# Norm squares summed by VectorE, an earlier memory load, and dt computed by feature in a three-layer float32 kernel

## The chip, the cores and the metric

The kernel runs on one core of one Trainium2 chip. The metric is the device time of one execution in microseconds (us); lower is better. TensorE multiplies, VectorE, ScalarE and GpSimd do the elementwise work, and SyncE issues the transfers. The profile calls them PE (with PEld for its weight loads), DVE, ACT, POOL and SP.

## The reference

The input is x, 512 tokens of 1024 features, and two memories of 256 tokens. A first block adds three branches to the residual stream h, each after an RMS norm: a mixer (a projection, a causal convolution of width 4, a chunked state space scan with 16 heads, and a multi-scale pooling), a cross attention on the memory, and a SwiGLU feed-forward. Two more layers (a convolution layer and a sparse attention layer) follow a final norm. All is float32.

```python
def rmsnorm(x, g):
    xf = x.astype(jnp.float32)
    y = xf * lax.rsqrt(jnp.mean(xf * xf, axis=-1, keepdims=True) + EPS)
    return (y * g.astype(jnp.float32)).astype(x.dtype)
...
    proj = u @ w_in
    z, xbc, dt_raw, v = jnp.split(
        proj, [SSD_INNER, SSD_INNER + CONV_DIM, SSD_INNER + CONV_DIM + SSD_HEADS], axis=-1)
...
    dt = jax.nn.softplus(dt_raw.astype(jnp.float32) + dt_bias.astype(jnp.float32))
...
    for l in range(DEPTH):
        h = h + hybrid_mixer(rmsnorm(h, mix_norm[l]), w_in[l], conv_w[l], conv_b[l], dt_bias[l],
                             a_log[l], d_skip[l], ssd_norm[l], pool_w[l], pool_scale[l], w_out_mix[l])
        h = h + memory_cross_attention(rmsnorm(h, xattn_norm[l]), rmsnorm(mem, mem_norm[l]),
                                       w_q[l], w_kv[l], w_o[l])
        h = h + swiglu(rmsnorm(h, ffn_norm[l]), w_gate_up[l], w_down[l])
    return rmsnorm(h, final_norm)
```

## The kernel before

The stream h is kept transposed in hT: features on the 128 partitions, 8 tiles of 512 tokens. Every large product is done in split precision. A weight tile of 1024 rows and 256 columns (1 MB) is loaded into w_raw in two halves, GpSimd splits it into w_hi (one instruction, L613) and w_lo (four, L628), and TensorE multiplies w_hi by the high part of the input, w_hi by its low part and w_lo by its high part. Such a tile with its products is a job. Jobs are numbered in one list, JOBS, and run strictly in that order: kv1_k (4), kv1_v (4), xbc (6), dt (1), v (4), z (4), pool (1), wo_pool (4), wo_ssd (4), q1 (4) and so on.

There are two slots for weights. SyncE loads tile j once tile j-2 is split (slot_free), GpSimd splits tile j once job j-2 has been used up (w_used), and TensorE starts job j once tile j is split (w_split) and the output bank of job j-2 has been emptied (g_free). A job with 512 tokens has 48 matmuls of 512 columns, one on the memory 48 of 256 columns. products_as_ready (L711) is the form that takes its input tile by tile as the low part appears; products_T (L698) and products_nat (L720, output by token) take it whole. The other results of TensorE go through four banks of t_bank in the order of the list TASKS.

The opening: SyncE issues 21 small parameter transfers into p_rows, then mem (1 MB), then x (2 MB), then three broadcasts, then the weight tiles of kv1_k. ScalarE waits for mem and all parameters, squares mem for its norm (L1185), VectorE scales mem (L1794), TensorE transposes it, ScalarE writes m_hi and VectorE m_lo (L1802), which counts m1_lo. TensorE then transposes x (L796), sums the squares of x (statistic, L752), and only then runs the kv1_k jobs.

The norm of h needs the sum over all 1024 features, that is over partitions as well. ScalarE squares each of the 8 tiles into a ring of two buffers (nring), and TensorE multiplies a matrix of ones by each square, accumulating: 8 tiles, each of which the trace shows as two float32 matmuls. For the first norm that is L752, for the other three (stat2, stat3, stat4) squares_sum (L766), two tiles after each output job and the last two after the first job of the next stage. ScalarE takes the root, VectorE the reciprocal and applies it.

The dt job is a product by token with only 16 columns: x is the stationary operand, in 96 matmuls of 16 columns. VectorE turns its output into dt and adt, and then runs the four pooling windows (window, L1853 to L1869), for which the v jobs deliver the input.

Of the kernel before, what the change touches and what calls it, by code (L numbers as in the profile page):

```python
# [20 lines left out]
ALU = mybir.AluOpType  # L21
ACT = mybir.ActivationFunctionType
# [4 lines left out]
P = 128  # L27
D = 1024
DT = D // P
T = 512  # L30
# [89 lines left out]
def slot_tasks(s):  # L120
# [7 lines left out]
    [("params", 2), ("mem1", 4), ("x", DT), ("stat1", 1), ("xbcT", XS + GROUPS), ("acs", 1), ("cb", 2), ("abc0", 4)]  # L128
# [62 lines left out]
def program(nc, A, out):  # L191
    with ExitStack() as ctx:
        def sem(name):
            return ctx.enter_context(nc.semaphore(name))
# [48 lines left out]
        mean = at("mean", [P, T], rN + 2 * KB)  # L243
        nring = at("nring", [P, 2, T], rN + 4 * KB)
# [28 lines left out]
        dt_, adt, acs, eacs, dtd, cdec = sm  # L273
        t1, t2, t3 = [at(n, [P, CHUNKS, HEADS], rM + 8 * KB + 256 * i) for i, n in enumerate(("t1", "t2", "t3"))]
# [116 lines left out]
        xs_ready = sem("xs_ready")  # L391
        dtx, sp_e, sp_l, adt_ready = sem("dtx"), sem("sp_e"), sem("sp_l"), sem("adt_ready")
# [43 lines left out]
        def _(sp):  # L436
# [26 lines left out]
            for s, rows in enumerate(PARAM_SETS):  # L463
                r = 0
                for name, arr, n in rows:
                    if len(A[arr].shape) == 1:
                        v = A[arr].rearrange("(r c) -> r c", c=P)
                    elif len(A[arr].shape) == 2:
                        v = A[arr].rearrange("a (r c) -> (a r) c", c=P)
                    else:  # L470
                        v = A[arr].rearrange("a t (r c) -> (a t r) c", c=P)
                    if s >= 2:
                        v = v[(s - 2) * n:(s - 1) * n, :]
                    sp.dma_start(p_rows[r:r + n, s, :], v).then_inc(in_small, 16)
                    r += n
# [4 lines left out]
            stream(JOBS["kv1_k"], 4, w_cols("w_kv", 0))  # L480
# [203 lines left out]
        def _(pe):  # L684
# [72 lines left out]
            def sq(k):  # L757
                return nring[:, k % 2, :]

            def squares_sum(i, nth, k0, k1):  # L760

                if k0 == 0:
                    bank(i)
                for k in range(k0, k1):
                    pe.wait_ge(sq_ready, nth * DT + k + 1)
                    last = nc.tensor.matmul(t_bank[:, BANK[i], :], ones[:], sq(k), start=(k == 0), stop=(k == DT - 1))  # L766
                    if k < DT - 1:
                        last.then_inc(sq_used, 1)
                    else:
                        last.then_inc(t_ready, 1)  # L770
# [21 lines left out]
            pe.wait_ge(in_x, 16)  # L792
            for k in range(DT):
                b = bank(TASKS["x"] + k)
                for m in range(TT):
                    last = nc.tensor.transpose(b[:, m * P:(m + 1) * P], x_nat[:, m, k * P:(k + 1) * P], ident[:])  # L796
                last.then_inc(t_ready, 1)
            statistic(TASKS["stat1"], DT, sq, (sq_ready, 0), sq_used)
# [112 lines left out]
            for i in range(1, 4):  # L911
                jobs(JOBS["wo_ssd"] + i, 1, lambda par: products_T(par, x_hi, x_lo))
                squares_sum(TASKS["stat2"], 1, 2 * i - 2, 2 * i)
            products_as_ready(JOBS["q1"], y_hi, y_lo, lambda k: pe.wait_ge(nlo_ready, DT + k + 1))
            squares_sum(TASKS["stat2"], 1, 6, 8)
# [40 lines left out]
            for i in range(1, 4):  # L956
                jobs(JOBS["wo1"] + i, 1, lambda par: products_T(par, y_hi, y_lo))
                squares_sum(TASKS["stat3"], 2, 2 * i - 2, 2 * i)

            products_as_ready(JOBS["gu0"], x_hi, x_lo, lambda k: pe.wait_ge(nlo_ready, 2 * DT + k + 1))  # L960
            squares_sum(TASKS["stat3"], 2, 6, 8)
            f0 = 0
            for c, n in enumerate(FF_CHUNKS):
                first = 1 if c == 0 else 0
                jobs(JOBS[f"gu{c}"] + first, n - first, lambda par: products_T(par, x_hi, x_lo))
                products_as_ready(JOBS[f"down{c}"], y_hi, y_lo, lambda k: pe.wait_ge(ff_lo, f0 + k + 1), kt=n)
                if c < 2:
                    jobs(JOBS[f"down{c}"] + 1, 3, lambda par: products_T(par, y_hi, y_lo, kt=n))
                else:
                    for i in range(1, 4):  # L970
                        jobs(JOBS[f"down{c}"] + i, 1, lambda par: products_T(par, y_hi, y_lo, kt=n))
                        squares_sum(TASKS["stat4"], 3, 2 * i - 2, 2 * i)
                f0 += n
            jobs(JOBS["kvb_k"], 1, lambda par: products_T(par, m_hi, m_lo, n=MEM))
            squares_sum(TASKS["stat4"], 3, 6, 8)
# [168 lines left out]
        def _(act):  # L1144
# [17 lines left out]
            def squares(n, used0, ready_wait):  # L1162
                for k in range(n):
                    ready_wait(k)
                    if k >= 2:
                        act.wait_ge(sq_used, used0 + k - 1)
                    nc.scalar.activation(nring[:, k % 2, :], hT[:, k, :], ACT.Square).then_inc(sq_ready, 1)

# [11 lines left out]

            act.wait_ge(in_mem1, 16)
# [23 lines left out]
            for k in range(DT):  # L1205
                i = TASKS["x"] + k
                b = ready(i)
                copy(hT[:, k, :], b).then_inc(h_tile, 1)
                act.wait_ge(h_tile, k + 1)
                act.nop().then_inc(t_free[BANK[i]], 1)  # L1210
            squares(DT, 0, lambda k: None)
            root(TASKS["stat1"])

# [3 lines left out]

            for i in range(4):
                norm_hi(0, 2 * i)
                norm_hi(0, 2 * i + 1)  # L1220
                j = JOBS["kv1_k"] + i
                act.wait_ge(w_used, j + 1)
                copy(k1[:, 2 * i:2 * i + 2, :], g_bank[:, 2 * (j % 2):2 * (j % 2) + 2, 0:MEM]).then_inc(g_free[j % 2], 1)
            for i in range(4):
# [61 lines left out]

            act.wait_ge(dtx, 1)
# [3 lines left out]
            raw_pair(0, JOBS["v"])  # L1291
# [65 lines left out]
            def square(nth, k):  # L1357
                if k >= 2:
                    act.wait_ge(sq_used, nth * (DT - 1) + k - 1)
                nc.scalar.activation(nring[:, k % 2, :], hT[:, k, :], ACT.Square).then_inc(sq_ready, 1)  # L1360
# [363 lines left out]
        def _(dve):  # L1724
# [35 lines left out]
            def add_to_residual(base, n=4):  # L1760

                for i in range(n):
                    j = base + i
                    dve.wait_ge(w_used, j + 1)
                    for f in range(2):
                        k = 2 * i + f
                        ins = v.tensor_tensor(hT[:, k, :], hT[:, k, :], g_bank[:, 2 * (j % 2) + f, :], ALU.add)  # L1767
                        if f == 0:
                            ins.then_inc(h_done, 1)
                        else:  # L1770
                            done(ins, h_done, g_free[j % 2])

# [33 lines left out]
            dve.wait_ge(t_ready, TASKS["x"] + DT)  # L1806
# [3 lines left out]
            dve.wait_ge(h_tile, DT)  # L1810
# [17 lines left out]
            j = JOBS["dt"]  # L1828
            dve.wait_ge(w_used, j + 1)
            g = g_bank[:, 2 * (j % 2):2 * (j % 2) + 2, :].rearrange("p b (m c) -> p (b m) c", c=WC)[:, :, 0:HEADS]  # L1830
            done(v.tensor_tensor(t3[:], g, bc[:, 0:1, :].to_broadcast([P, CHUNKS, HEADS]), ALU.add), g_free[j % 2])
# [192 lines left out]

            def residual_and_lo(base, nth, gain, hi, lo):

                for i in range(4):
# [9 lines left out]
                    for k in (2 * i, 2 * i + 1):  # L2037
                        dve.wait_ge(nhi_ready, nth * DT + k + 1)
                        v.scalar_tensor_tensor(lo[:, k, :], hT[:, k, :], gain(k), hi[:, k, :].bitcast(F32),
                                               ALU.mult, ALU.subtract).then_inc(nlo_ready, 1)  # L2040

# [44 lines left out]
            for c, n in enumerate(FF_CHUNKS):  # L2086
# [13 lines left out]
                add_to_residual(JOBS[f"down{c}"])  # L2100
# [300 lines left out]
```

## Time and profile before

| | |
|---|---|
| median of 3 runs | 1885.59 us (1884.83 to 1888.43) |
| profiled execution | 1885.64 us, its span 1883.6 us |
| mean granted TensorE clock | 0.972 of full speed |
| busy: PE, DVE, ACT, POOL | 94%, 50%, 27%, 57% |

The span is the time between the first and the last instruction that the profiler saw, and 2.0 us lie around it. Times in rows are counted from the span's start.

### The profile page before, as it was taken

The numbers are of one execution on the slowest core, as the hardware profiler recorded it, in microseconds if no ns is written. First come the engines' busy times: TensorE is split into PE (matmuls) and PEld (weight loads), VectorE is DVE, ScalarE is ACT, GpSimd is POOL, SyncE is SP. The second block draws the span as 40 slices with busy tenths as digits, with TensorE's granted clock in tenths as the row PEclk, the third lists the DMA queues.
The fourth block names the chain that finished last, engine by engine and source line by source line (L and its number), as shares of the span: only waits on it lengthen the run. The fifth ranks groups of instructions, "written<-read, shape, count | busy, mean of one in ns | idle before, by whom it ended". The sixth has DMA issues, their size and how long they took to land.

```text
span 1883.6 us, 23072 instructions
## 1 busy us (share of the span) xinstructions
PE 1769.3 (94%) x8317; PEld 1433.4 (76%) x8317; DVE 937.1 (50%) x1455; ACT 514.2 (27%) x876; POOL 1077.5 (57%) x781
## 2 busy tenths in 40 slices
PE   4899999899999999999999999998898989999995
PEld 3778897687787788888878877875676768777783
DVE  2547674665232331221219998997314676452313
ACT  4122223232031210110112435645102234554103
POOL 3976664236554666666777787672762544334550
PEclk9998999899999999999999999999898999999998
DMA  4332222112232233333234332221231222121211
GB/s 163 112 112 69 68 90 67 45 68 67 92 130 57 80 111 90 89 112 90 78 102 128 95 89 90 68 89 46 67 82 43 90 68 68 45 68 45 90 45 45
DMA packets 188503, 153.14 MB, mean 81 GB/s; under 512 B 9412, under 2 KB 186112, under 8 KB 188416
## 3 DMA queue, kind: packets, MB, share of 16 engines
q1 hardware_dynamic: 188416, 151.95, 26.0%
q8 instruction: 58, 0.95, 0.2%
q14 instruction: 29, 0.24, 0.0%
HBM read 148.79 MB, written 2.10 MB: 80 GB/s over the span
## 4 chain that ended last, share of the span: by engine, by line
PE 77%; DVE 12%; issue 5%; ACT 3%; POOL 2%; DMA 1%; DVEq 1%; SPq 0%; ACTq 0%; POOLq 0%
PE g_bank L698 49%; PE g_bank L711 7%; PE g_bank L720 6%; DVE t_bank L2145 4%; PE t_bank L752 2%; PE t_bank L1102 1%; PE t_bank L1092 1%; PE t_bank L888 1%; POOL w_lo L628 1%; PE t_bank L766 1%; PE g_bank L1046 1%; PE t_bank L838 1%; POOL w_hi L613 1%; DVE isc L2285 1%; PE t_bank L934 1%
## 5 line engine op out<-in xcount | busy, mean ns | idle before, releaser
L628 POOL TENSOR_TENSOR w_lo<-w_raw,w_hi 128x512 fp32r<-128x512 f32 x480 | 653.9, 1393 | 10.0
L613 POOL TENSOR_SCALAR w_hi<-w_raw 128x2048 fp32r<-128x2048 f32 x120 | 244.5, 2038 | 668.5 <-issue 292.7
L698 PE MATMUL g_bank<-x_hi,w_hi 128*128 128x512 f32 x1248 | 494.3, 396 | 3.0 <-DVEq L1738 3.0
L698 PE MATMUL g_bank<-x_hi,w_lo 128*128 128x512 f32 x1248 | 487.1, 390 | 0.0
L698 PE MATMUL g_bank<-x_lo,w_hi 128*128 128x512 f32 x1248 | 487.1, 390 | 0.0
L698 PEld LDWEIGHTS g_bank<-x_hi,w_hi 128*128 128x128 f32 x1248 | 235.1, 188 | 55.2 <-issue 7.4
L698 PEld LDWEIGHTS g_bank<-x_lo,w_hi 128*128 128x128 f32 x1248 | 235.1, 188 | 49.7 <-issue 1.7
L698 PEld LDWEIGHTS g_bank<-x_hi,w_lo 128*128 128x128 f32 x1248 | 234.9, 188 | 49.3
L2145 DVE SCALAR_TENSOR_TENSOR t_bank<-hc,cols,t_bank 128x512 f32<-128x512 f32 x280 | 186.2, 747 | 2.4 <-DVE hc L2123 2.4
L646 POOL TENSOR_TENSOR w_lo<-w_raw,w_hi 128x512 fp32r<-128x512 f32 x80 | 100.9, 1294 | 63.9 <-ACT w_hi L1457 63.9
L698 PE MATMUL g_bank<-y_hi,w_hi 128*128 128x512 f32 x332 | 132.1, 398 | 1.4 <-ACTq L1326 1.4
L698 PE MATMUL g_bank<-y_hi,w_lo 128*128 128x512 f32 x332 | 129.4, 390 | 0.0
L698 PE MATMUL g_bank<-y_lo,w_hi 128*128 128x512 f32 x332 | 129.3, 390 | 0.0
L2235 DVE SCALAR_TENSOR_TENSOR hT<-hT,g_bank 128x512 f32<-128x512 f32 x32 | 20.5, 683 | 131.7 <-PE g_bank L698 111.9
L2092 DVE TENSOR_TENSOR gs<-g_bank,rstd 128x512 f32<-128x512 f32 x22 | 15.2, 691 | 140.2 <-PE g_bank L698 140.0
L1435 ACT ACTIVATE sg<-gs 128x512 f32<-128x512 f32 x22 | 13.9, 632 | 253.7 <-DVE gs L2092 253.7
L698 PEld LDWEIGHTS g_bank<-y_hi,w_hi 128*128 128x128 f32 x332 | 62.4, 188 | 15.9 <-issue 2.8
L698 PEld LDWEIGHTS g_bank<-y_lo,w_hi 128*128 128x128 f32 x332 | 62.4, 188 | 13.8 <-issue 1.2
L698 PEld LDWEIGHTS g_bank<-y_hi,w_lo 128*128 128x128 f32 x332 | 62.3, 188 | 13.1
L662 POOL TENSOR_TENSOR pacc<-pacc,prod 128x512 f32<-128x512 f32 x54 | 68.2, 1296 | 5.9 <-ACT prod L1146 5.9
L1767 DVE TENSOR_TENSOR hT<-hT,g_bank 128x512 f32<-128x512 f32 x24 | 15.4, 684 | 99.0 <-PE g_bank L698 82.0
L2311 DVE CUSTOM_DVE_ANT_0 pB<-t_bank,mask 128x128 f32<-128x128 f32 (+3 forms) x48 | 23.6, 491 | 76.4 <-PE t_bank L1092 69.0
(357 smaller groups left out, 2948.5 us busy)
## 6 DMA issues: line engine op xcount, KB each, us to landing
w_raw<-w_gate_up SPq DMA_DIRECT2D x44, 512.0 KB, 4.6
w_raw<-a_w_in SPq DMA_DIRECT2D x44, 512.0 KB, 4.4
w_raw<-b_w_in SPq DMA_DIRECT2D x38, 512.0 KB, 4.4
w_raw<-w_in SPq DMA_DIRECT2D x28, 512.0 KB, 4.3
w_raw<-w_kv SPq DMA_DIRECT2D x16, 512.0 KB, 4.3
w_raw<-w_out_mix SPq DMA_DIRECT2D x16, 512.0 KB, 4.4
w_raw<-w_down SPq DMA_DIRECT2D x16, 512.0 KB, 4.4
w_raw<-a_w_out SPq DMA_DIRECT2D x16, 512.0 KB, 4.1
```

Of the source, the lines that this page charges most:

```text
L613: nc.gpsimd.tensor_scalar(w_hi[:, par], w_raw[:, par], 1.0, 0.0, ALU.mult, ALU.add).then_inc(pool_chain, 1)
L628: last = nc.gpsimd.tensor_tensor(w_lo[:, par, s], w_raw[:, par, s], w_hi[:, par, s].bitcast(F32), ALU.subtract)
L646: last = nc.gpsimd.tensor_tensor(w_lo[:, par, s], w_raw[:, par, s], w_hi[:, par, s].bitcast(F32), ALU.subtract)
L662: nc.gpsimd.tensor_tensor(acc_k[:], acc_k[:], p[:], ALU.add).then_inc(tap_chain, 1)
L698: last = nc.tensor.matmul(g_bank[:, 2 * pair + f, 0:n], ww[:, par, k0 + k, ws], xk, start=(k == 0 and q == 0), stop=(k == kt - 1 and q == 2))
L711: last = nc.tensor.matmul(g_bank[:, 2 * par + f, :], ww[:, par, k, ws], xx[:, k0 + k, :], start=(k == 0 and q == 0), stop=(k == kt - 1 and ...
L720: last = nc.tensor.matmul(g_bank[:, 2 * par + m // 2, m % 2 * WC:m % 2 * WC + n], xx[:, k, m * P:(m + 1) * P], ww[:, par, k, 0:n], start=( ...
L752: last = nc.tensor.matmul(b, ones[:], src(k), start=(k == 0), stop=(k == n - 1))
L766: last = nc.tensor.matmul(t_bank[:, BANK[i], :], ones[:], sq(k), start=(k == 0), stop=(k == DT - 1))
L2145: ins = v.scalar_tensor_tensor(tail if k == TAPS - 1 else a(k), h(k), wk, a(k), ALU.mult, ALU.add)
L2235: ins = v.scalar_tensor_tensor(hT[:, k, :], hT[:, k, :], 1.0 if half else ALPHA, g_bank[:, 2 * (j % 2) + f, :], ALU.mult, ALU.add)
L2311: ins = v.tensor_tensor_reduce(p_unit(u, i), b[:, i % per * W_OF[1]:i % per * W_OF[1] + w], mask[:, M_AT[qb]:M_AT[qb] + w], SLOPES[4 * hg ...
```

## The change

1. The memory is transferred first, then the weight tiles of kv1_k jobs 0 and 1, then x and the broadcasts; SyncE issues these. The 21 parameter transfers are issued by ScalarE's queue.
2. TensorE's order is kv1_k 0 and 1, the transposes of x tiles 0 to 3, kv1_k 2, x tiles 4 to 7, kv1_k 3, and the first norm's sum.
3. For all four norms ScalarE writes the first square to sq_sum and the others to the ring; VectorE adds the seven others to sq_sum, and TensorE does one product of ones with sq_sum. For stat2, stat3 and stat4 it stands where the last two tiles' products stood.
4. dt is computed by feature: w (16 columns) is the stationary operand and x moves, in 24 matmuls of 512 columns; ScalarE copies the 16 rows to dtT, and behind the first v job TensorE transposes them back (four transposes, task dtT). ScalarE's evacuation of the first v job stands ahead of its two dt activations.

```diff
-    [("params", 2), ("mem1", 4), ("x", DT), ("stat1", 1), ("xbcT", XS + GROUPS), ("acs", 1), ("cb", 2), ("abc0", 4)]
+    [("params", 2), ("mem1", 4), ("x", DT), ("stat1", 1), ("xbcT", XS + GROUPS), ("dtT", 1), ("acs", 1), ("cb", 2), ("abc0", 4)]
...
             sp.dma_start(mem1[:], A["mem"][0].rearrange("(m p) d -> p m d", p=P)).then_inc(in_mem1, 16)
+            k_cols = w_cols("w_kv", 0)
+            for i in range(2):
+                load(i, i, k_cols(i * WC))
             sp.dma_start(x_nat[:], A["x"][0].rearrange("(m p) d -> p m d", p=P)).then_inc(in_x, 16)
...
+            def squares_sum(i, nth):
+
+                b = bank(i)
+                pe.wait_ge(sq_used, (nth + 1) * (DT - 1))
+                nc.tensor.matmul(b, ones[:], sq_sum[:], start=True, stop=True).then_inc(t_ready, 1)
...
             pe.wait_ge(m1_lo, DT)
-            jobs(JOBS["kv1_k"], 4, lambda par: products_T(par, m_hi, m_lo, n=MEM))
+            kv1_k(0)
+            kv1_k(1)
+            x_T(0, 4)
+            kv1_k(2)
+            x_T(4, 8)
+            kv1_k(3)
+            b = bank(TASKS["stat1"])
+            pe.wait_ge(sq_used, DT - 1)
+            nc.tensor.matmul(b, ones[:], sq_sum[:], start=True, stop=True).then_inc(t_ready, 1)
...
-            jobs(JOBS["dt"], 1, lambda par: products_nat(par, x_hi, x_lo, TT, n=HEADS))
+            j = JOBS["dt"]
+            slot(j, j % 2, j // 2)
+            for k in range(KT):
+                for q, (ww, xx) in enumerate(((w_hi, x_hi), (w_hi, x_lo), (w_lo, x_hi))):
+                    last = nc.tensor.matmul(g_bank[0:HEADS, 2 * (j % 2), :], ww[:, j % 2, k, 0:HEADS], xx[:, k, :],
+                                            start=(k == 0 and q == 0), stop=(k == KT - 1 and q == 2))
+            last.then_inc(w_used, 1)
...
-            jobs(with_v, 2, lambda par: products_T(par, x_hi, x_lo))
+            jobs(with_v, 1, lambda par: products_T(par, x_hi, x_lo))
+            pe.wait_ge(dt_moved, 1)
+            b = bank(TASKS["dtT"])
+            for c in range(CHUNKS):
+                last = nc.tensor.transpose(b[:, c * HEADS:(c + 1) * HEADS], dtT[0:HEADS, c * P:(c + 1) * P], ident[0:HEADS, 0:HEADS])
+            last.then_inc(t_ready, 1)
+            jobs(with_v + 1, 1, lambda par: products_T(par, x_hi, x_lo))
...
+            for k in range(1, DT):
+                dve.wait_ge(sq_ready, k + 1)
+                v.tensor_tensor(sq_sum[:], sq_sum[:], nring[:, k % 2, :], ALU.add).then_inc(sq_used, 1)
+                dve.wait_ge(sq_used, k)
...
+            def add_squares(nth, i):
+
+                for k in (2 * i, 2 * i + 1):
+                    dve.wait_ge(sq_ready, nth * DT + k + 1)
+                    if k:
+                        v.tensor_tensor(sq_sum[:], sq_sum[:], nring[:, k % 2, :], ALU.add).then_inc(sq_used, 1)
+                        dve.wait_ge(sq_used, nth * (DT - 1) + k)
```

## Rows read from the trace of the kernel before

**Rows 1.** The page's head and its first part (busy us, share, instructions).

```profile
span 1883.6 us, 23072 instructions
PE 1769.3 (94%) x8317; PEld 1433.4 (76%) x8317; DVE 937.1 (50%) x1455; ACT 514.2 (27%) x876; POOL 1077.5 (57%) x781
```

**Rows 2.** The chain that ended last, opening (start us, us, what).

```profile
32.69 9.06 PE t_bank L752 x16
41.75 9.96 PE g_bank L698 x84
...
103.26 11.23 PE g_bank L711 x48
```

**Rows 3.** Timeline of POOL, opening: tiles 1, 3 and 9.

```profile
26.05 1.90 POOL L613 TENSOR_SCALAR w_hi<-w_raw 128x2048 fp32r<-128x2048 f32 x1 [21.91 <-DMA w_raw<-w_kv]
...
47.70 2.31 POOL L613 TENSOR_SCALAR w_hi<-w_raw 128x2048 fp32r<-128x2048 f32 x1 [7.82 <-PE g_bank L698]
...
98.19 5.02 POOL L628 TENSOR_TENSOR w_lo<-w_raw,w_hi 128x512 fp32r<-128x512 f32 x4
```

**Rows 4.** Timeline of the opening on SP, PE, ACT and DVE.

```profile
8.44 0.41 SPq L476 DMA_DIRECT2D mem<-mem  x1
11.91 0.98 PE L778 MATMUL t_bank<-ident,p_rows 116*128 116x116 f32 x4 [11.91 <-DMA p_rows<-a_conv_w]
14.24 1.06 ACT L1185 ACTIVATE x_hi<-mem 128x1024 fp32r<-128x1024 f32 x1 [1.11 <-DMA mem<-mem]
18.41 1.42 DVE L1794 TENSOR_SCALAR mem<-mem,mstat 128x1024 f32<-128x1024 f32 x2
26.33 1.11 DVE L1802 SCALAR_TENSOR_TENSOR m_lo<-t_bank,cols,m_hi 128x256 fp32r<-128x256 f32 x2 [0.32 <-DVE m_lo L1802]
68.60 3.47 DVE L1788 TENSOR_TENSOR x_lo<-nring,x_hi 128x512 fp32r<-128x512 f32 x2
```

**Rows 5.** DMA issues (issues, KB each, median us to landing).

```profile
w_raw<-w_kv SPq DMA_DIRECT2D x16, 512.0 KB, 4.3
mem<-mem SPq DMA_DIRECT2D x2, 1024.0 KB, 5.4
```

**Rows 6.** Timeline of DVE: one instruction with POOL splitting, and without.

```profile
115.21 1.67 DVE L1823 TENSOR_SCALAR acc<-raw,cols 128x512 f32<-128x512 f32 x1 [43.14 <-ACT raw L1146]
...
170.39 0.53 DVE L1823 TENSOR_SCALAR acc<-raw,cols 128x512 f32<-128x512 f32 x1
```

**Rows 7.** The chain, dt job, v jobs 0 and 1, v jobs 2 and 3.

```profile
174.68 17.97 PE g_bank L720 x96
192.65 24.23 PE g_bank L698 x96
...
217.28 21.86 PE g_bank L698 x96
```

**Rows 8.** Windows, dt job (busy us of PE, PEld, DVE, ACT, POOL; PEclk; DMA share; GB/s).

```profile
178.00:182.00 4.00, 4.00 (x20) 4.00 (x21) 3.93 (x3) 0.00 (x0) 4.00 (x3) 0.50 0.00 0
```

**Rows 9.** Timeline of DVE: end of adt, first and last row of the four windows.

```profile
200.22 0.23 DVE L1842 SCALAR_TENSOR_TENSOR adt<-dt__95,bc 128x64 f32<-128x64 f32 x1
206.71 0.08 DVE L1853 MEMSET wbuf<- 128x30 f32 x1 [6.27 <-ACT raw L1146]
...
261.56 1.48 DVE L1869 TENSOR_TENSOR y_lo<-acc,y_hi 128x512 fp32r<-128x512 f32 x2
```

**Rows 10.** The chain, stat2: two pairs of tiles and a 512-token job.

```profile
436.77 1.96 PE t_bank L766 x4
438.73 10.91 PE g_bank L698 x48
449.63 1.72 PE t_bank L766 x4
```

**Rows 11.** Timeline of POOL, second kvb_k tile, and the chain, first a_glu job.

```profile
980.27 1.90 POOL L613 TENSOR_SCALAR w_hi<-w_raw 128x2048 fp32r<-128x2048 f32 x1 [2.90 <-issue]
1012.95 11.34 PE g_bank L711 x48
```

More of the change, by code:

```diff
@@ L479, in _ @@
                 sp.dma_start(bc[:, i, :], A[n][0].partition_broadcast(P)).then_inc(in_bc, 16)
-            stream(JOBS["kv1_k"], 4, w_cols("w_kv", 0))
+            for i in range(2, 4):
+                slot_free(i)
+                load(i, i % 2, k_cols(i * WC))
             stream(JOBS["kv1_v"], 4, w_cols("w_kv", D))
@@ L791, in _, with x_T, kv1_k @@
                 last.then_inc(t_ready, 1)
[L792 to L798, printed above, removed]
-            pe.wait_ge(m1_lo, DT)
-            jobs(JOBS["kv1_k"], 4, lambda par: products_T(par, m_hi, m_lo, n=MEM))
+            def x_T(k0, k1):
+                pe.wait_ge(in_x, 16)
+                for k in range(k0, k1):
+                    b = bank(TASKS["x"] + k)
+                    for m in range(TT):
+                        last = nc.tensor.transpose(b[:, m * P:(m + 1) * P], x_nat[:, m, k * P:(k + 1) * P], ident[:])
+                    last.then_inc(t_ready, 1)
+            def kv1_k(i):
+                j = JOBS["kv1_k"] + i
+                slot(j, j % 2, j // 2 if j >= 2 else None)
+                products_T(j % 2, m_hi, m_lo, n=MEM).then_inc(w_used, 1)
+            pe.wait_ge(m1_lo, DT)
+            kv1_k(0)
[7 more added lines that the diff above has]
+            nc.tensor.matmul(b, ones[:], sq_sum[:], start=True, stop=True).then_inc(t_ready, 1)
             jobs(JOBS["kv1_v"], 4, lambda par: products_nat(par, m_hi, m_lo, MT))
@@ L910, in _ @@
                 last.then_inc(t_ready, 1)
-            for i in range(1, 4):
-                jobs(JOBS["wo_ssd"] + i, 1, lambda par: products_T(par, x_hi, x_lo))
-                squares_sum(TASKS["stat2"], 1, 2 * i - 2, 2 * i)
+            jobs(JOBS["wo_ssd"] + 1, 4 - 1, lambda par: products_T(par, x_hi, x_lo))
             products_as_ready(JOBS["q1"], y_hi, y_lo, lambda k: pe.wait_ge(nlo_ready, DT + k + 1))
-            squares_sum(TASKS["stat2"], 1, 6, 8)
+            squares_sum(TASKS["stat2"], 1)
             jobs(JOBS["q1"] + 1, 4 - 1, lambda par: products_T(par, y_hi, y_lo))
@@ L966, in _ @@
                 products_as_ready(JOBS[f"down{c}"], y_hi, y_lo, lambda k: pe.wait_ge(ff_lo, f0 + k + 1), kt=n)
[L967 to L972, printed above, removed]
+                jobs(JOBS[f"down{c}"] + 1, 3, lambda par: products_T(par, y_hi, y_lo, kt=n))
                 f0 += n
             jobs(JOBS["kvb_k"], 1, lambda par: products_T(par, m_hi, m_lo, n=MEM))
-            squares_sum(TASKS["stat4"], 3, 6, 8)
+            squares_sum(TASKS["stat4"], 3)
             jobs(JOBS["kvb_k"] + 1, 1, lambda par: products_T(par, m_hi, m_lo, n=MEM))
@@ L1204, in _, with k1_evac, x_and_squares @@
                     copy(m_hi[:, k, :], b[:, kk * MEM:(kk + 1) * MEM], col["mem_norm"](k)).then_inc(m1_hi, 1)
[L1205 to L1212, printed above, removed]
+            def k1_evac(i):
+                j = JOBS["kv1_k"] + i
+                act.wait_ge(w_used, j + 1)
+                copy(k1[:, 2 * i:2 * i + 2, :], g_bank[:, 2 * (j % 2):2 * (j % 2) + 2, 0:MEM]).then_inc(g_free[j % 2], 1)
+            def x_and_squares(k0, k1):
+                for k in range(k0, k1):
+                    i = TASKS["x"] + k
+                    b = ready(i)
+                    copy(hT[:, k, :], b).then_inc(h_tile, 1)
+                    act.wait_ge(h_tile, k + 1)
+                    act.nop().then_inc(t_free[BANK[i]], 1)
+                    if k >= 3:
+                        act.wait_ge(sq_used, k - 2)
+                    dst = nring[:, k % 2, :] if k else sq_sum[:]
+                    nc.scalar.activation(dst, hT[:, k, :], ACT.Square).then_inc(sq_ready, 1)
             def norm_hi(base, k):
@@ L1771, in add_to_residual @@
                             done(ins, h_done, g_free[j % 2])
+                    if nth is not None:
+                        add_squares(nth, i)
             def rms_apply(nth, gain):
```

91 lines of the change are left out of this document (42 added, 49 removed).

## The prediction

> **What bounds the kernel now.** I read the page's head first: PE is busy for 94% of the span, POOL for 57%, DVE for 50% [rows 1]. So work taken off TensorE counts where TensorE is the last to finish, and I went to the chain of waits to find where it isn't. In the opening the chain runs over the sum of squares, then kv1_k jobs 0 and 1, and it reaches the first xbc job at 103.26 [rows 2]. Between these TensorE needs only 6 us for a memory job, but POOL needs 7 us for a tile, and up to 9 where DVE works beside it. POOL's timeline shows that it started its third tile at 47.70, when kv1_k 0 had been used up, and ended the ninth, that of xbc 0, at 103.2: seven tiles in 55.5 us with one gap under 1 us [rows 3]. The opening is bound by POOL, and its clock starts with the first kv1_k job. From 103 us to the end of the feed-forward TensorE sets the pace in most places: a 512-token job takes 10.9 us [rows 10], a tile's split 7 to 8.5.
>
> **The opening (about 13 us less).** TensorE could not start kv1_k 0 before 41.75 - 0.6, because the transposes and squares of x stood ahead of it. Its own inputs were there earlier: m_lo was done at 27.4 [rows 4], and tile 0 was split only at 33 (26.05 and the 7 us of a split) because its weights stood behind mem, x and the broadcasts in SP's queue (POOL waited until 26.05) [rows 3].
> Afterwards mem is issued at about 0.8 in place of 8.44 [rows 4] and lands at 0.8 + 5.4 = 6.2 [rows 5]; tiles 0 and 1 follow it at some 4.3 us each [rows 5], so at about 11 and 15. Their splits take 7 us each: 11 to 18, 18 to 25.
> The parameters: SP issued 21 of them in 7.6 us, and the last landed at 11.9 [rows 4]. ScalarE's queue issuing such transfers is not in this trace; I take SP's price for it, so ScalarE can square mem at 12.0 in place of 14.24, 2.2 us earlier. From below the price is nothing; from above it is 0.6 us an issue (twice SP's), and then the parameters land at 16 and ScalarE starts 2 us later than before. Other transfers now run beside them, which pulls towards late.
> Against that, POOL now splits while DVE scales mem. DVE's one-input instruction took 1.67 us with POOL at work and 0.53 without [rows 6], 1.1 more; the two at L1794 [rows 4] and a small reciprocal then cost some 2.9 us in all. The m_lo instructions read a PSUM bank and one SBUF tensor, and the two at 26.33 took no longer with POOL splitting from 26.05 on [rows 3, 4]. So m_lo is done at 27.4 - 2.2 + 2.9 = 28.1, and TensorE starts there.
> The Trainium skill (SBUF - State Buffer, section "SBUF: two separate sides") says that the port pair of DVE and GpSimd is locked for a whole instruction by whichever comes first. The trace agrees, as the 1.67 against 0.53 us shows; without this rule the start would be 25.2 and the gain 3 us more.
> kv1_k 0 ends at 34.1, and POOL begins the third tile at 34.3, 13.4 us earlier than 47.70. Then seven tiles follow. As before, three of them run beside DVE's norm; the seven additions of squares touch two more, for which I add 0.5. So xbc 0 starts at 90, 13 us earlier. Is x ready? Tile transposes go between the kv1_k jobs. With splits at 41.3 and 49, kv1_k 3 ends near 56, the sum takes 0.9, and from the end of the sum to the last x_lo the kernel before took 72.1 - 41.75 = 30.3 us [rows 2, 4], so 87. That is 3 us of margin to 90, and products_as_ready gives 8 more. The weights of kv1_k 2 stand behind x and should land near 27, needed at 34.3. The removed part, seven of eight sums, lies off POOL's path and counts nothing here by itself. Bounds: 9 us (parameters late by 4) to 16.5 (no lock).
>
> **dt by feature (about 8 us less).** The job took 17.97 us [rows 7], at half clock (1.2 GHz) from 178 on [rows 8], with 16-column matmuls and PEld busy throughout. 24 matmuls of 512 columns cost 24/48 x 10.9 = 5.5 us [rows 10]. TensorE would reach v 0 at 180.1, but POOL has that tile split only at 182.0: it can start when xbc 5 has been used, at 173.8, ahead of the transposes before 174.68, and a split beside DVE takes some 8 us. So 10.6 us are left. v 0 and 1 took 24.23 where v 2 and 3 took 21.86 [rows 7]: the slow clock ran into them, and 2.4 us more come back. Transposes cost 0.3. That makes 12.7 us on TensorE.
> What is late next is DVE. Before, dt's small instructions were over at 200.4, and the windows waited for v 0 until 206.7 [rows 9]. Now v 0 is ready at 193.0, but dt's eight instructions come only behind the transposes and take the same 7.8 us, so the windows start at 201.5: 5.2 us earlier. They run 56.3 us nearly without a gap (206.7 to 263.0) [rows 9]; two gaps of 1.9 us in all, for which TensorE was late, close. ScalarE's copies of v wait for free ring buffers, and the z jobs wait for these copies, so the end of the windows sets z 2. I get 7 to 8.5 and take 8. Bounds: 4 (more lock time) and 12.7.
>
> **stat2, stat3, stat4 (7.4 + 6.0 + 3.7 us less).** Two tiles cost 1.72 us on TensorE, and there are 12 such pairs; the first one took 1.96, behind 1.1 of waiting for the square (the job ahead of it ended at 435.6) [rows 10]. One tile stays, 0.86 us. For stat2 that is 1.1 + 1.96 + 3 x 1.72 - 0.86 = 7.4, for stat3 4 x 1.72 - 0.86 = 6.0. DVE gets seven additions each. None of these stands in the trace; the nearest is a two-input instruction at 0.69 alone and up to 1.8 beside POOL. They stand behind the low parts that TensorE waits for. The last pair is done some 8 us after the last output job, and TensorE wants it after 10.9, so the cover is q1 0, gu0 0 or kvb_k 0. Without it the two last additions would cost 3.5 us each time. I take 0.
> For stat4 the cover matters: behind it come four memory tiles and POOL is last again, from 980.27 to a_glu 0 at 1012.95 [rows 11]. The first three pairs, 5.2 us, stand ahead of that run and let it start 3.5 us earlier (the tile before it, 7 us, is then the limit); the fourth is hidden. With the norm's apply a little more beside POOL I take 3.7. Bounds for all three: 11 to 18.5.
>
> **Sum.** 13 + 8 + 7.4 + 6.0 + 3.7 = 38.1. The profiled execution took 1885.64 us with a span of 1883.6, 0.05 over the median, so 1885.6 - 38.1 = 1847.5 us.
>
> **Rivals.** (a) Parameters late. The small transfers on ScalarE's queue share the engines with 3 MB of weights and mem and land at 16 or later; the opening gives 5 to 9, the total 30 to 34: 1851 to 1856. For it: this trace has no transfer that ScalarE issues. Against it: they are small.
> The Trainium skill (DMA: Bandwidth & Descriptors, "Issuing engines are not separate DMA queues") says that transfers from all issuers run on the same 16 engines and interleave, and that a second issuer saves only issue time. No run here shows it yet; by it alone the opening's gain would come from the order, and case (a) gets its chance.
> (b) dt gives TensorE's full 12.7 and the lock costs nothing: 38.1 + 4.7 + 3 = 46, 1840. For it: POOL splits fewer tiles at the places where DVE is late. Against it: rows 9.
> (c) The additions are exposed. DVE's sums come later than the cover, TensorE waits about 3.5 us in each of three norms and the first norm reaches xbc 0 late by 3: 14 less gain, 1861. Against it: 3 us of margin computed.
> (d) Slower than before. It has one mechanism: the squares of mem wait for parameters that land behind x. Everything in the opening moves with that landing. TensorE's start is 16 us behind it, so a landing at 25 us gives the opening's gain back, and slower than before needs one past 50. Before, mem, x and tile 0, 4 MB in all, were in at 26 us [rows 3].
>
> **How the numbers follow.** Main case 0.5, (a) 0.2, (b) 0.15, (c) 0.12, (d) and the like 0.03. The range 1837 to 1859 takes in (a) and (b) and the nearer half of (c), and leaves out 2 in 10. About 0.2% (3.8 us) is what a measurement of this kernel can tell from no change; faster by more has 0.96, within it 0.01, slower 0.03.
>
> **What would show it.** TensorE's first kv1_k matmul at 28 (25 if no lock, over 31 for case a); POOL's third tile at 34; xbc 0 at 90; x_lo done before that; the dt job 5.5 us at full clock with a short wait for POOL behind it; the windows starting 5 us earlier relative to the dt job; one pair of matmuls for each norm, with no wait ahead of it; a_glu 0 still behind POOL. The prediction is wrong if TensorE waits for x_lo at xbc 0, if the 16-column product lowers the clock as the old one did, or if ScalarE's issues take over 0.6 us each.

## The result and the profile after

The changed kernel takes 1858.68 us (median of 4 runs, 1857.81 to 1861.51) against 1886.61 us for the kernel before on the same chip (4 runs, 1884.83 to 1888.43): a ratio of 0.9855, with a 95% interval from 0.9837 to 0.9872. The gain is 27 to 28 us where 38 was forecast. The time is 11 us over the number 1847.5 and 0.3 us inside the upper end of the range. The profiled execution took 1859.07 us, 26.6 less than the one before.

The head of the page, to be held against [rows 1]: TensorE has 38 us less work, DVE 44 us more.

```profile
span 1857.1 us, 22885 instructions
PE 1730.9 (93%) x8193; PEld 1405.7 (76%) x8193; DVE 981.5 (53%) x1483; ACT 514.5 (28%) x877; POOL 1089.1 (59%) x781
```

The chain that ended last, opening of the changed kernel (start us, us, what), to be held against [rows 2]:

```profile
8.95 12.19 DMA p_rows<-a_conv_w
21.19 1.28 ACT L1198
...
26.66 1.42 DVE mem L1827 x2
28.12 1.13 PE t_bank L778 x4
...
35.77 13.26 PE g_bank L693 x96
...
66.35 1.10 PE t_bank L805 x2
...
102.08 11.19 PE g_bank L706 x48
```

The chain now runs over the landing of the parameters; before, it ran over that of mem (8.44 to 14.22). ScalarE's last of 21 issues began at 8.95, 0.9 us later than SyncE's before (8.04), but the last parameters landed 12.2 us behind that. The first kv1_k job started at 35.8, forecast was 28.1; xbc 0 at 102.1, forecast was 90, before it was 103.3. So nearly the whole term of the opening is gone.

ScalarE's queue and the large transfers ahead of it (timeline of issues; last line: issue, KB, us to landing; SyncE issued x from 4.30 on, so it was in at 19.2):

```profile
0.81 0.63 ACTq L1192 DMA_DIRECT2D p_rows<-mix_norm  x1
...
8.19 1.13 ACTq L1192 DMA_DIRECT2D p_rows<-a_conv_w  x3
```

```profile
x_nat<-x SPq DMA_DIRECT2D x1, 2048.0 KB, 14.9
```

POOL's timeline in the opening (start us, us, instruction, in brackets what it waited for), tiles 1, 3, 4 and 9, to be held against [rows 3]:

```profile
16.30 1.90 POOL L608 TENSOR_SCALAR w_hi<-w_raw 128x2048 fp32r<-128x2048 f32 x1
...
43.48 1.92 POOL L608 TENSOR_SCALAR w_hi<-w_raw 128x2048 fp32r<-128x2048 f32 x1 [20.26 <-PE g_bank L693]
...
52.47 6.22 POOL L623 TENSOR_TENSOR w_lo<-w_raw,w_hi 128x512 fp32r<-128x512 f32 x4
...
95.80 6.22 POOL L623 TENSOR_TENSOR w_lo<-w_raw,w_hi 128x512 fp32r<-128x512 f32 x4
```

The third tile starts 4.2 us earlier than in [rows 3], 7.7 us behind the first kv1_k matmul. From there POOL needs 58.6 us to the start of xbc 0, where it needed 55.6 before (103.26 - 47.70). POOL has no idle time between 43.48 and 101.99: TensorE did wait 1.6 us for the sum of the first norm (66.35), but that held nothing up, and the last x_lo was done at 99.7, 2.4 us ahead of xbc 0. DVE's additions lie beside the splits; the first, which began as POOL went from w_hi to w_lo, is the only short one:

```profile
52.17 0.75 DVE L1841 TENSOR_TENSOR sq_sum<-sq_sum,nring 128x512 f32<-128x512 f32 x1 [16.52 <-ACT nring L1234]
53.49 2.84 DVE L1841 TENSOR_TENSOR sq_sum<-sq_sum,nring 128x512 f32<-128x512 f32 x2 [0.56 <-ACT nring L1234]
58.88 7.32 DVE L1841 TENSOR_TENSOR sq_sum<-sq_sum,nring 128x512 f32<-128x512 f32 x4 [2.56 <-ACT nring L1234]
```

The dt stage. Window 176 to 182 (busy us of PE, PEld, DVE, ACT, POOL; PEclk; DMA share; GB/s), then DVE's last dt instruction and the first row of its windows, to be held against [rows 8, 9]:

```profile
176.00:182.00 6.00, 4.09 (x18) 1.91 (x16) 5.89 (x5) 0.50 (x1) 6.00 (x5) 1.00 0.00 0
```

```profile
199.76 0.23 DVE L1876 SCALAR_TENSOR_TENSOR adt<-dt__96,bc 128x64 f32<-128x64 f32 x1
199.94 0.08 DVE L1887 MEMSET wbuf<- 128x30 f32 x1
```

The clock is full through the dt job. TensorE's job v 0 starts at 180.97 behind a POOL wait of 1.9 us, and the windows start right behind dt's instructions: DVE is what is late next, as forecast. The norms, in the chain (start us, us, what), to be held against [rows 10, 11]:

```profile
446.22 10.88 PE g_bank L706 x48
457.10 0.86 PE t_bank L759 x2
...
591.53 10.88 PE g_bank L706 x48
602.41 0.86 PE t_bank L759 x2
...
976.86 7.51 PE g_bank L715 x48
984.40 1.49 POOL w_lo L623
985.93 11.19 PE g_bank L706 x48
```

One product stands directly behind the job that was to cover the additions, with no wait ahead of it, and a_glu 0 is still behind POOL.

How far each landmark moved, before minus after: xbc 0 by 1.2; z 2 by 11.2 (267.53 to 256.30); q1 1 by 18.7 (476.64 to 457.96); the second gu0 job by 24.8 (628.11 to 603.27); a_glu 0 by 27.0. The differences of these are the measured terms: 1.2 for the opening, 10.0 for dt, 15.6 for the three norms (7.3 + 6.2 + 2.2; the first is counted from wo_ssd 0, which moved by 11.4, 0.2 more than z 2). Some 75 us before the end the lead is 25.25 (1809.28 to 1784.03), at the end 26.5.

### The profile page after: what moved, and what is told of

Read it like the earlier page. It is cut to its first block, busy times and chain, and to the rows that moved or that the text cites. A ratio compares the mean times of both kernels' runs of the same rounds, so it can differ in the third digit from the quotient of the medians.

```text
span 1857.1 us, 22885 instructions
## 1 busy us (share of the span) xinstructions
PE 1730.9 (93%) x8193; PEld 1405.7 (76%) x8193; DVE 981.5 (53%) x1483; ACT 514.5 (28%) x877; POOL 1089.1 (59%) x781
## 3 DMA queue, kind: packets, MB, share of 16 engines
q1 hardware_dynamic: 187664, 151.66, 26.5%
## 4 chain that ended last, share of the span: by engine, by line
PE 71%; DVE 15%; issue 5%; ACT 3%; POOL 3%; DMA 1%; DVEq 1%; ACTq 0%; POOLq 0%
PE g_bank L693 48%; PE g_bank L706 7%; PE g_bank L715 4%; DVE t_bank L2188 4%; PE t_bank L747 2%; POOL w_lo L623 2%; PE t_bank L1109 1%; PE t_bank L1099 1%; POOL w_hi L608 1%; PE t_bank L904 1%; PE g_bank L1053 1%; PE t_bank L854 1%; DVE isc L2328 1%; PE t_bank L948 1%; PE t_bank L967 1%
## 5 line engine op out<-in xcount | busy, mean ns | idle before, releaser
L623 POOL TENSOR_TENSOR w_lo<-w_raw,w_hi 128x512 fp32r<-128x512 f32 x480 | 665.4, 1417 | 10.0
L641 POOL TENSOR_TENSOR w_lo<-w_raw,w_hi 128x512 fp32r<-128x512 f32 x80 | 101.0, 1298 | 64.4 <-ACT w_hi L1488 64.4
L693 PEld LDWEIGHTS g_bank<-y_lo,w_hi 128*128 128x128 f32 x332 | 62.3, 188 | 12.9 <-issue 0.2
```

The lines of the kernel that those rows point to most:

```text
L623: last = nc.gpsimd.tensor_tensor(w_lo[:, par, s], w_raw[:, par, s], w_hi[:, par, s].bitcast(F32), ALU.subtract)
L641: last = nc.gpsimd.tensor_tensor(w_lo[:, par, s], w_raw[:, par, s], w_hi[:, par, s].bitcast(F32), ALU.subtract)
L693: last = nc.tensor.matmul(g_bank[:, 2 * pair + f, 0:n], ww[:, par, k0 + k, ws], xk, start=(k == 0 and q == 0), stop=(k == kt - 1 and q == 2))
```

## The experiments

Each run has 4 executions or more, unless said otherwise. Executions of one and the same kernel differ by up to 9.5 us here, and the time goes with the mean granted clock: the run e1 below gave 1851.94 and 1852.60 us at a mean clock of 0.980 and 0.978, 1859.83 and 1861.33 at 0.976 and 0.975. So medians that are 3 us apart tell nothing by themselves, and what an experiment did to the opening is read from its trace. Even the unchanged opening puts xbc 0 at 103.26 in the trace before, 102.06 in e5 and 104.82 in e6, so the 1.2 us that the opening gained between the two traces lie within that spread.

### When do the parameters land (e1, e2, e3, e11)

e1: the loop of 21 transfers is taken from ScalarE and put ahead of mem on SyncE.

```diff
+            [the loop over PARAM_SETS, with sp.dma_start]
             sp.dma_start(mem1[:], A["mem"][0]...).then_inc(in_mem1, 16)
```

> The changed kernel with the 21 parameter transfers issued by SyncE again, ahead of mem, the two weight tiles and x. Theory Q (a small transfer lands only behind the bytes that were issued before it, whoever issues it): the parameters land at about 12, as in the kernel before; tile 0 lands 8.6 us behind the issue of mem, at 17, and is split at 24; VectorE scales mem beside that split, 2 us slower; kv1_k 0 starts at 29 to 30 in place of 35.8, xbc 0 at about 96, and the time is 6 us less than the changed kernel's, 1852 to 1853 us. Rival S (ScalarE's queue is slow by itself, or the landing isn't what binds): with S the landing is early too, since SyncE issues; with a start not bound by the landing kv1_k 0 stays past 34 and the time at 1857 to 1859.

e2: SyncE waits behind mem.

```diff
             sp.dma_start(mem1[:], A["mem"][0]...).then_inc(in_mem1, 16)
+            sp.wait_ge(in_small, 16 * sum(len(s) for s in PARAM_SETS))
             k_cols = w_cols("w_kv", 0)
```

> The changed kernel, ScalarE still issues the parameters, but SyncE waits for all of them behind mem, and only then issues the weight tiles and x. Theory Q: only 1 MB is ahead of the parameters, they land at 12 to 13 in place of 21.2, kv1_k 0 starts at 27 to 29, the time is 7 to 8 us less than the changed kernel's, 1851 us. Rival S (transfers of ScalarE's queue take long by themselves, about 12 us from the last issue): they land at 20 or later, the tiles at 24 and 29, kv1_k 0 at 36 or later, and the time is 1859 to 1865.

e3: the same line, but behind the two tiles and ahead of x.

> As the one before, but the weight tiles are issued at once and only x (2 MB) waits for the parameters. Theory Q: 3 MB are ahead, at 370 GB/s from 1 us on these are in at about 10 to 12, the parameters at 12 to 14, kv1_k 0 starts at 28 to 30, the time is 1851 to 1853. Rival R (the queues share the engines packet by packet, so what counts is that any load is on the engines at all): the parameters land later than in the run where the tiles wait too, but by the share alone, and the three landings don't follow the bytes ahead. Rival S: 20 or later.

e11: SyncE issues the parameters, behind x and ahead of the broadcasts (one execution).

> The changed kernel with the parameter transfers issued by SyncE again, but behind mem, the two tiles and x (ahead of the broadcasts). Theory Q: one queue or two, what counts is the bytes ahead. SyncE's last issue comes at about 12, the parameters land with x or up to 3 us behind, at 20 to 22; kv1_k 0 near 36, about 1858 to 1861. Rival T (ScalarE's queue was what made them late): with SyncE issuing they land 3.5 us behind the last issue, at 15 to 16, and kv1_k 0 starts at 31.

Each kernel's first instruction that uses the parameters, on TensorE (start us, us, instruction, wait), for e1, e2, e3 and e11 in this order:

```profile
12.89 0.98 PE L780 MATMUL t_bank<-ident,p_rows 116*128 116x116 f32 x4 [12.89 <-DMA p_rows<-a_conv_w]
```

```profile
11.90 0.98 PE L768 MATMUL t_bank<-ident,p_rows 116*128 116x116 f32 x4 [11.90 <-DMA p_rows<-a_conv_w]
```

```profile
14.69 0.98 PE L768 MATMUL t_bank<-ident,p_rows 116*128 116x116 f32 x4 [14.69 <-DMA p_rows<-a_conv_w]
```

```profile
22.65 0.98 PE L780 MATMUL t_bank<-ident,p_rows 116*128 116x116 f32 x4 [22.65 <-DMA p_rows<-a_conv_w]
```

| kernel | issued by | ahead of the last one | landed | first kv1_k | xbc 0 | median us |
|---|---|---|---|---|---|---|
| e2 | ScalarE | 1 MB | 11.9 | 28.5 | 95.8 | 1855.78 |
| e1 | SyncE | nothing | 12.9 | 30.6 | 97.1 | 1856.22 |
| e3 | ScalarE | 3 MB | 14.7 | 30.6 | 97.1 | 1856.23 |
| changed kernel | ScalarE | 5 MB | 21.2 | 35.8 | 102.1 | 1858.68 |
| e11 | SyncE | 5 MB | 22.7 | 37.2 | 104.3 | 1863.36 |

Theory Q gives the landings. With the same issuer and the same 21 transfers, the landing comes later with more bytes ahead, though not in proportion: 2.8 us from 1 to 3 MB, and 6.5 from 3 to 5 MB, which would be x at 320 GB/s. S falls with e2 (ScalarE's queue delivers within 3.4 us of the start of the last issue when little is ahead) and T falls with e11 (SyncE's own transfers landed 8.3 us behind the start of their last issue, at 14.25, where T wants 3.5; landing, kv1_k 0 and time all came a little later than expected there).

The packets show that this is not one queue for all. Below are the changed kernel's queues from 12 to 14 us and from 18 to 20 us (q1 is SyncE's, q10 ScalarE's: packets, MB, share), then all packets of e11 from 12 to 16 us:

```profile
q1 hardware_dynamic: 189, 0.76, 98.8%
q10 hardware_dynamic: 45, 0.02, 3.7%
...
q1 hardware_dynamic: 643, 0.55, 87.0%
q10 hardware_dynamic: 235, 0.12, 25.8%
```

```profile
DMA packets 401, 1.64 MB, mean 411 GB/s; under 512 B 0, under 2 KB 0, under 8 KB 401
```

The small packets of ScalarE's queue went along beside x's, 45 to 189, and faster once x's were through; 495 of the 752 had gone by 18 us. So they did not wait for the 5 MB to be in: they shared the engines with them and were slowed, which is the mechanism of rival R in e3, though R did not expect the landings to follow the bytes. In e11, where SyncE issued them behind x, no packet under 2 KB moved in these 4 us: within one queue they did stand behind. The landing of e1 fits the sharing too. It had nothing ahead, but mem and the tiles right behind it (from 8.45 on), and was 1.0 us later than e2's. What sets the proportion between the two queues no run shows. The Trainium skill (DMA: Bandwidth & Descriptors, "Issuing engines are not separate DMA queues") says that transfers of all issuers run on the same 16 engines and that a second issuer saves issue time only; e2, e3 and e11 agree. The same page, section "Queues, rings and completion order", says that an engine takes packets in turn from the rows that it has work for; the two queues' packets in one stretch agree with that, though not one for one.

The times agree less well than the landmarks: 1851 to 1853 was expected of the three, and their fastest executions gave 1851.9, 1853.2 and 1851.8, but the medians are only 2 to 3 us under the changed kernel's, and the ratios to the kernel before (0.9857, 0.9847 and 0.9855 for e1, e2 and e3) can't be told from its 0.9855. The changed kernel's four executions all had a mean clock of 0.978 to 0.980; the five of e1 to e3 that had such a clock took 1851.8 to 1853.2 us, some 6 less. That agrees with the landmarks, but they ran on another chip and are picked by their clock, so the gain is shown up to xbc 0 and not for the whole kernel.

### What else stands between the landing and xbc 0 (e9, e8, e10)

e9: ScalarE squares mem before it waits for the parameters; the squares need only mem.

```diff
             act.wait_ge(in_mem1, 16)
-            act.wait_ge(in_small, 16 * sum(len(s) for s in PARAM_SETS))
             act.wait_ge(const_ready, 1)
             [squares of mem, root]
+            act.wait_ge(in_small, 16 * sum(len(s) for s in PARAM_SETS))
```

> The changed kernel with one edit: ScalarE squares mem before it waits for the parameters; x isn't held back. Theory: the parameters land at 21.2 as in the changed kernel, but only their own transposes, the copies and m_hi and m_lo are left behind them. In the run with both edits the first kv1_k matmul came 12.1 us behind the landing, of which 4.4 was the wait for VectorE's scaling; here scaling is over by then, so 12.1 - 3.2 = 9 us behind 21.2: kv1_k 0 at 30 in place of 35.8, the third tile at 38, xbc 0 at 96.5, and about 5 us less than the changed kernel's profile, 1853 to 1855. Rival (the landing is what binds, not the squares): 35 and 1858.

It measured 29.7, 37.6 and 96.1, and 1853.32 us (1851.28 to 1858.66; the ratio, 0.9851, can't be told from the changed kernel's either). The landing stayed at 21.07, so 6 us of the chain behind it were work that never needed it.

e8: e9 and e3 together.

> The changed kernel with x waiting for the parameters, and ScalarE squaring mem as soon as mem is there, before it waits for the parameters. The squares need only mem. Theory: the parameters land at 14.6, but table load, squares and root (5.4 us) are over by then, VectorE scales mem from 14.5 on, kv1_k 0 starts at 25 in place of 30.6, the third tile at 33 in place of 38.6, xbc 0 at 91 to 92 in place of 97, and the profiled time is 5 to 6 us under that of the run where x alone waits: 1846 to 1848. Rival (the opening is bound by another thing at once: x or the weights of kv1_k 2, which now land behind the parameters, or the norm's apply): xbc 0 at 95 or later, 1851 or more.

Its landing was 14.57, and the first kv1_k at 26.65, 1.7 later than expected: VectorE's scaling, 2.9 us in e3, took 4.0 here, beside the end of POOL's split of tile 1 and the start of tile 2's. The third tile came at 35.4 and xbc 0 at 93.97, where 91 to 92 was expected; 1852.29 us (1848.06 to 1854.44), where 1846 to 1848 was. The rest of the third tile's delay is TensorE's clock, granted at 0.50 from 26 to 32 us. TensorE's first rows of kv1_k 0 in e8, at 0.41 us a matmul from the second on:

```profile
26.65 0.58 PE L694 MATMUL g_bank<-m_hi,w_hi 128*128 128x256 f32 x1 [4.10 <-DVEq L1770]
27.03 0.41 PE L694 MATMUL g_bank<-m_lo,w_hi 128*128 128x256 f32 x1
```

e10: e8, and TensorE gets work while it would be idle.

```diff
+            for _ in range(24):
+                nc.tensor.matmul(g_bank[:, 0, 0:P], ones[:], ones[:], start=True, stop=True)
             pe.wait_ge(in_small, 16 * sum(len(s) for s in PARAM_SETS))
...
+            for _ in range(2):
+                nc.tensor.matmul(g_bank[:, 0, :], ones[:], mem1[:, 0, 0:T], start=True, stop=True)
             pe.wait_ge(m1_lo, DT)
```

> The run with both edits (x waits, squares first), and TensorE runs 24 small products of ones with ones ahead of the parameters, and two of 512 columns behind the transposes of mem, into a bank that kv1_k 0 then overwrites; nothing reads them. In the run without them kv1_k 0 began at 26.65 with 0.41 us matmuls (half clock), and the third tile started 8.8 us behind it, where at full clock the job takes 6.0. Theory: the idle TensorE is what halves the clock of kv1_k 0; with work ahead it takes 6 to 6.5 us, the third tile starts at 33 to 33.5 in place of 35.4, xbc 0 2 us earlier at 92, 1849 to 1851 median. Rival 1: such little work doesn't raise the clock, 35.4 stays, 1852. Rival 2: POOL or the norm takes the 2 us back before xbc 0.

TensorE and POOL in e10 (timelines):

```profile
22.43 1.88 PE L800 MATMUL g_bank<-mem,ones 128*128 128x512 f32 x4
26.66 0.38 PE L694 MATMUL g_bank<-m_hi,w_hi 128*128 128x256 f32 x1 [2.35 <-DVEq L1774]
26.88 0.28 PE L694 MATMUL g_bank<-m_lo,w_hi 128*128 128x256 f32 x1
```

```profile
32.88 1.92 POOL L609 TENSOR_SCALAR w_hi<-w_raw 128x2048 fp32r<-128x2048 f32 x1 [9.11 <-PE g_bank L694]
```

The job starts at the same 26.66, runs at 0.28 us a matmul from the start (granted clock 1.00 from 26 to 32 us) and is used up 2.6 us earlier; xbc 0 comes at 91.4, 2.6 earlier. In e1, e3 and e9, too, kv1_k 0 began at 0.41 us a matmul, for 3.8 to 4.2 us, while the profile gives the granted clock as 1.00: there the duration of a matmul shows the slow start and the clock of the profile does not. The time is 1846.92 us (5 runs, 1843.08 to 1851.32), ratio 0.9806 (0.9782 to 0.9829). This is the lowest median of all: 0.5% or 9 us below the changed kernel by the two ratios, and its interval doesn't touch the other. It is e3, e9 and the warm start in one. The warm start's own part is shown by the traces up to xbc 0 only: e8's ratio, 0.9817 (0.9800 to 0.9834), overlaps e10's.

### The additions beside POOL (e4)

e4 leaves out the seven additions of the first norm, so its sum is the first square alone; the semaphores are counted as before.

```diff
                 dve.wait_ge(sq_ready, k + 1)
-                v.tensor_tensor(sq_sum[:], sq_sum[:], nring[:, k % 2, :], ALU.add).then_inc(sq_used, 1)
-                dve.wait_ge(sq_used, k)
+                dve.nop().then_inc(sq_used, 1)
```

> The changed kernel without VectorE's seven additions of squares in the first norm (left out, so the first norm's sum is the first square alone; the semaphores are counted as before). Theory L (the additions lock GpSimd out where it splits the tiles that bound the opening): the seven tiles from 43.5 take 56 to 57 us in place of 58.5, and the time is 1.5 to 3 us less, 1856 to 1857. Rival (the loss comes from the norm's apply, which now runs beside more splits): the tiles take 58 us and the time is that of the changed kernel within 0.7 us.

POOL in e4, third tile, and the first instruction of the tile behind that of xbc 0:

```profile
43.73 1.90 POOL L608 TENSOR_SCALAR w_hi<-w_raw 128x2048 fp32r<-128x2048 f32 x1 [20.51 <-PE g_bank L693]
45.71 5.04 POOL L623 TENSOR_TENSOR w_lo<-w_raw,w_hi 128x512 fp32r<-128x512 f32 x4
...
52.71 5.04 POOL L623 TENSOR_TENSOR w_lo<-w_raw,w_hi 128x512 fp32r<-128x512 f32 x4
...
99.31 1.91 POOL L608 TENSOR_SCALAR w_hi<-w_raw 128x2048 fp32r<-128x2048 f32 x1
```

The seven tiles take 55.6 us (43.73 to 99.31), as in the kernel before; with the additions they take 58.5 (43.48 to 101.99). Theory L stands in the trace: seven additions on VectorE cost POOL 2.9 us where POOL is last, and since POOL had no idle time in either kernel, it isn't TensorE's wait for the sum that cost them. The profiled execution was 3.06 us shorter (1856.01), but the median, 1859.01, shows nothing; at this size the runs' spread hides it. The Trainium skill (SBUF - State Buffer, section "SBUF: two separate sides") says that an instruction of VectorE with two SBUF inputs and one of GpSimd shut each other out for their whole length; 0.75 us for the first addition against 1.4 to 2.2 for the later ones, and 6.2 against 5.0 us for the four w_lo instructions, agree.

### Each part alone (e5, e6, e7)

These are the kernel before with the hunks of one part of the diff in the section on the change: its item 4 (e5), its item 3 for norms 2 to 4 (e6), and its items 1, 2 and the first norm (e7).

> The kernel before with the dt part alone (opening and all four norms as before). By the two traces the start of z 2 moves by 10.0 us more than xbc 0 does, where 8 was predicted from VectorE's windows starting 5.2 us earlier. If that is the price of this part alone: 1874 to 1876 us. Rival: part of the 10 us belongs to the opening (POOL's lead going into the dt job); then this run gives 8 or less, 1877 or more. For TensorE's full saving of 12.7 it would be 1872.

> The kernel before with VectorE's additions and the one product in norms 2, 3 and 4 alone (opening, first norm and dt as before). Theory: TensorE's pairs go away and the additions are covered by the job behind: 7.3 + 6.2 + 2.2 = 15.7 us, read from the two traces (predicted 17.1), so 1868 to 1870 us. Rival (the additions cost something later, where GpSimd is locked out): 12 us or less, 1873 or more.

> The kernel before with the new opening alone (order of loads, ScalarE's queue, order of TensorE, additions in the first norm). Theory Q with the lock: the parameters land at 21, kv1_k 0 starts near 36, the seven tiles take 58.5 us, xbc 0 starts at 102: 1 us less than before, 1883 to 1885 us. Rival (the opening's 1.2 us is only what was left of a larger gain that the other parts hid): 1880 or less.

| part | forecast | by the two traces | alone, medians | ratio alone |
|---|---|---|---|---|
| opening | 13 | 1.2 | 1.7 (1883.42, 10 runs) | 0.9990 (0.9980 to 0.9999) |
| dt | 8 | 10.0 | 12.0 (1873.18, 4 runs) | 0.9937 (0.9921 to 0.9954) |
| norms 2 to 4 | 17.1 | 15.6 | 14.5 (1870.60, 4 runs) | 0.9919 (0.9902 to 0.9936) |
| sum | 38.1 | 26.8 | 28.2 | |

The differences are to the 1885.14 us of the kernel before in these comparisons. The parts add up to the whole, so nothing was lost between them. The shortfall is in the opening, 11 to 12 us; the norms lack another 1.5 to 2.6, and dt gives 2 to 4 more than its term. Two chain rows of e5, xbc 0 and z 2, and two of e7, the dt job in its old form and z 2:

```profile
102.06 11.23 PE g_bank L713 x48
...
257.78 17.27 PE g_bank L722 x144
```

```profile
173.14 15.27 PE g_bank L713 x96
...
262.78 12.23 PE g_bank L713 x102
```

From xbc 0 to z 2 the kernel before needs 164.3 us, e5 155.7: dt by feature gives 8.6 there, and 8 was forecast. The changed kernel gives 10.0. Both have dt's new form; the 1.4 between them is the first v job, which took 1.6 us more in e5 (changed kernel, then e5):

```profile
180.97 11.20 PE g_bank L693 x48
...
181.01 12.82 PE g_bank L700 x48
```

The granted clock from 182 to 186 us was 1.00 in the changed kernel and 0.57 in e5. The old form differs as well from one execution to the next: the dt job took 15.3 us in e7 and 18.0 in [rows 7], and from xbc 0 (101.74) to z 2 e7 needs 161.0 us, 3.3 less than the kernel before. Held against e7's trace dt would give 5.3 to 6.8, so 8.6 and 10.0 are figures of single pairs of traces.

## Why the prediction was wrong

**The step that failed** is in the opening: "I take SP's price for it, so ScalarE can square mem at 12.0". The price of an issue was nearly right (0.32 to 0.63 us each, the last one begun at 8.95). What was wrong is that the landing was counted from the last issue, as in [rows 4], where no large transfer had been issued ahead of it. In the changed kernel mem, the tiles and x were all issued by 6.1, ahead of the last parameters; x was in at 19.2, and the parameters, which had shared the engines with it, landed at 21.2 where 12.0 was forecast. Rival (a) named this mechanism, but gave it a landing of 16 and a chance of 0.2; the bytes that it needed for a better figure were in rival (d) (4 MB in by 26 us), without asking when 5 MB would be in if nothing held them back. e2, e3 and e11 show the cause; e1 and e3 give 5 us of it back at xbc 0. Rival (d) had the gain used up by a landing at 25. One at 21.2 nearly did it, because two losses that (d) left out came on top of it, the second and third below.

That the time still lies inside the range is luck. The opening's own bounds were 9 to 16.5, and it gave 1.2; what kept the total in was dt's surplus and the room made for rival (c), which did not happen as written.

How the 12.1 us by which xbc 0 missed its forecast of 90 divide: 7.7 for the start of kv1_k 0 (35.8 for 28.1), 1.5 because that job ran at half clock at first (7.7 us to the third tile for 6.2), 2.9 for the seven tiles (58.6 for 55.7).
- The first is the landing, 9.2 us late, and 1.3 for ScalarE's table load behind it (the row at 21.19), which the forecast had overlooked; less the 2.9 allowed for the lock on VectorE's scaling, since POOL was idle by then and the two instructions took 1.4 us.
- The second was not in the sum; the granted clock was 0.50 from 36 to 39 us. The kernel before kept TensorE busy with x and its squares up to kv1_k 0; the change leaves it idle there. e10 shows it, with 2.6 us.
- The third is the term "the seven additions of squares touch two more, for which I add 0.5", mis-sized by 2.4: e4 measured it as 2.9. The rest is rounding, since 34.3 + 55.5 + 0.5 is 90.3. Rival (c) had the additions as its subject, but looked for them as a wait of TensorE for the sum and not as a delay of POOL. A wait of 1.6 us for that sum there was, and it cost nothing. Its other half, exposed additions in the later norms, did not come: no wait stands ahead of any of the three products.

**dt** was right in its mechanism and its size: full clock in the job, POOL's wait behind it, VectorE's windows as what is late next, 5.6 us earlier relative to xbc 0 (6.8 in all, 5.2 forecast), and 8.6 to 10.0 us at z 2 against the trace before (5.3 to 6.8 against e7's). Alone it gave 12.0 by medians; where the rest of that comes from after z 2 is not settled, since the placing of the half-clock stretches differs between traces.

**The norms**: 7.3 and 6.2 measured for 7.4 and 6.0; stat4 gave 2.2 where 3.7 was forecast, with POOL last again as written. The 1.5 that are missing lie between two POOL-bound runs with more of VectorE's work beside them; that is argued from the rows and was not tried.

**Later** the lead shrinks from 27.0 to 25.25 us between a_glu 0 and the last jobs. The one row that shows 1.6 us of it is a job at 1254.44 that took 12.49 us where its like took 10.92 before, in a window at a granted clock of 0.83. Such stretches lie elsewhere in other traces, so I don't count it as a cost of the change; no run tried it.

## What to carry to other kernels

When a small transfer is put beside large ones, expect it to land about when the bytes issued before its last one are in, whoever issues it, even if its packets go along with them: hold the large ones back that aren't needed yet, and let nothing wait for the small ones that doesn't read them. When work is moved off TensorE onto VectorE, ask first whether GpSimd is last there, because the additions are paid by it. And work that is moved away from in front of a TensorE job may leave it cold: what fills the idle time can be worth more than it costs.

## What the runs showed of the hardware

- Small transfers on another engine's queue neither waited for the large ones nor passed them: beside x's packets 45 of theirs went to 189, and 752 packets with 0.29 MB in all landed 3.4 us behind the start of the last issue with 1 MB ahead, 5.7 with 3 MB and 12.2 with 5 MB. In SyncE's own queue, behind x, none moved from 12 to 16 us.
- Products that nobody reads made the opening 2.6 us shorter. Some 10 us of small ones between 4.2 and 24.3 us brought kv1_k 0 from 0.41 us a matmul to 0.28.
- One and the same kernel varied by 0.5% (e1), with the mean granted clock between 0.975 and 0.980. In e2, TensorE waited 3.0 us for POOL ahead of xbc 0, and the job then took 12.7 us in place of 11.2, with 0.63 us for each of its early matmuls and 0.39 for the later ones; in e4 it waited as long and the job took 11.2, so such a wait slows the job in some executions only.
- The 16-column form of dt took 15.3 us in e7 and 18.0 in the kernel before, with the granted clock at 0.50 from 179 to 192 us and from 178 to 197; the same product with 512 moving columns ran at full clock and took 5.5 us.
